# Five column tiles of each round moved between the attention units of the round before

## The chip, the core and the metric

The kernel runs on one core of one Trainium2 chip. The metric is the time of one execution on the device, in microseconds (us), lower is better; it is given as the median of several runs. The engines are TensorE (PE in the rows), VectorE (DVE), ScalarE (ACT), GpSimd (POOL) and the queue engine SyncE (SP). Each runs its own instructions in order; they meet at semaphores.

## What is computed

One layer of a hybrid decoder on 512 tokens of width 1024: three token mixing branches (dilated sliding-window attention, a convolution module, an mLSTM matrix memory) run on one input projection, are gated per channel and summed; then an output projection, a mixture of experts, a per-layer input embedding and a last norm. The change touches the token mixing alone. Attention has three dilations and eight slots of 64 channels; the convolution module is a gated input, a depthwise convolution of 31 taps, a LayerNorm and a swish; memory q and k pass a depthwise convolution of 4 taps. Cut to that:

```python
h = rmsnorm(x, g_mix[i])
proj = h @ w_in[i]
(q_a, k_a, v_a, u_conv, q_m, k_m, v_m, o_m, i_m, f_m, gate_pre) = jnp.split(proj, SPLIT_IDX, axis=-1)
y_att = dilated_attention(q_a, k_a, v_a)
y_conv = conformer_conv(u_conv, ...)
qk = jax.nn.silu(causal_dwconv(concat([q_m, k_m]), ...))
h_m = mlstm(q_c, k_c, v_m, i_m + ..., f_m + ...)
y_m = jax.nn.sigmoid(o_m) * h_m
gates = jax.nn.sigmoid(gate_pre).reshape(b, s, N_BRANCH, d)
merged = (gates[..., 0, :] * (y_att @ w_br_att[i])
          + gates[..., 1, :] * (y_conv @ w_br_conv[i])
          + gates[..., 2, :] * (y_m @ w_br_mlstm[i]))
x = x + merged @ w_out[i]
```

## The kernel before

The program has stages one behind the other: the first norm and its transposes (to 34 us of the profiled execution), four **rounds** (34 to 463), the **merge** of the three branches in eight tiles of 128 channels (to 671), the output projection and router (to 773), the experts (to 1033), and the last stage. The change touches the rounds and the start of the merge.

A round `r` computes 128 channels of every branch: two attention slots, 128 convolution channels, one memory head. Its parts, by engine:

- **Column tiles**, eight of them (`CM_ORDER`): TensorE multiplies 128 columns of `w_in` with all 512 tokens, into bank `PA` or `PB` by turns. Each product is split: the weights and `h` are given as a rounded high part and a low part (what rounding left), and three products are summed (`split_product`, L786 is `mm`), so a column tile is 8 x 3 = 24 matmuls of 512 columns. ScalarE rounds the weights (`round_cm`, L569, two buffers `cm_high`), VectorE subtracts to get the **low part** (`cm_tile`, L1219), and only then TensorE may start. Tile order: convolution gate, convolution input, memory q, memory k, three attention q, attention k.
- **Token tiles**, four: 128 tokens by 384 channels (attention v, output gate, memory v), again 24 matmuls, with weights `wtm` rounded by ScalarE (L605) and with a low part of 3072 columns.
- The **31 taps** of the depthwise convolution on VectorE (L1286), with the low parts of column tiles 4 to 7 and of the token weights laid between them at places fixed by `CM_TILES_AT` and `TM_TILE_AT`; behind them the memory convolution (L1294, L1298), eight instructions, and its swish (L1302).
- Eight **units** `u`, one for each slot and block of 128 queries: TensorE scores for three dilations (plain fp32), VectorE adds the bias and takes the maximum (L1326, L1331, `negmax_ready`), ScalarE the exponent (L619), GpSimd adds the three parts (L1621, L1623), TensorE turns them (L878), ScalarE copies (L613), TensorE multiplies with v. Units 0 to 3 have a token tile on TensorE behind their scores. Units 4 to 7 have instead one short matmul of memory scores, whose product with the weights is L1338.
- The **tail**: memory outputs (ten matmuls of 129 columns), the last turn and products, the memory rows on VectorE (L1349 to L1363), two sets of four transposes (L935, L939), copied out by ScalarE (L645, L647) into `yT`.
- GpSimd writes the ALiBi **bias** of the next round (L1607, six products) when ScalarE has done the output gate (`sgo_ready`, L642).

Round 0 is straight code on TensorE and a loop runs rounds 1 to 3; on VectorE and ScalarE a loop runs rounds 0 to 2 and the last is straight code. TensorE starts the column tiles of a round when the tail of the one before is done. VectorE makes the low parts of tiles 0 and 1 of the next round in units 4 and 5, so these alone are ready early. After round 3 the LayerNorm of the convolution branch runs: two means over channels as matmuls with `mean` (L786), subtraction (L1386), squares and root on ScalarE (L670, L672), reciprocal and four more steps on VectorE (L1393 to L1397), swish. The first merge tile is mixed with it: gate, mean, branch, gate, branch, gate, branch. The merge weights come by two loads, `wg` (1.5 MB) and `wb` (0.75 MB), on one semaphore; `wb` lies where `wtm` lies, so both loads are asked for when the last token tile is done, and ScalarE waits for both in unit 3 of round 3 before it rounds the first gate (L573).

## Time and profile before

| | us |
|---|---|
| median of three runs | 1118.33 |
| lowest, highest | 1117.27, 1120.91 |
| the profiled execution, its own time | 1119.16 |
| its span, first to last instruction | 1117.3 |
| TensorE busy | 979.6 (88%) |
| VectorE busy | 458.3 (41%) |
| ScalarE busy | 307.7 (28%) |
| GpSimd busy | 163.4 (15%) |

Busy TensorE is not TensorE at its peak: matmuls overlap, their ends are modelled, and a matmul at the lower clock is busy for longer. So the share of 88% is read together with the granted clock of each stretch, and with what stands between two matmuls. By stage the span divides into 34 us ahead of the rounds, 429 us of rounds, 208 us of LayerNorm end and merge, and 446 us behind them.

### The profile page before, as it was taken

The page shows a single profiled execution, that of the slowest core. Times are in us where ns is not written, and L with a number is a line of the kernel's source. Part 1 is how long each engine was busy: PE and PEld are TensorE (multiplying, and loading weights), DVE is VectorE, ACT ScalarE, POOL GpSimd, SP SyncE. Part 2 cuts the span into 40 slices and gives each one's busy share as a digit, 9 for nine tenths or more (in the row PEclk, how much of TensorE's full clock was granted, in tenths as well). Part 3 has the DMA queues.
Part 4 walks back from the last instruction along what each step waited for, and adds up shares of the span by engine and source line. Part 5 has one row for each costly group of instructions (what it writes and reads, how often), then busy time and mean ns, then how long its engine had stood idle before and what let it go on. Part 6 is the DMA issues. An engine that isn't in the chain of part 4 may idle for free.

```text
span 1117.3 us, 12509 instructions
## 1 busy us (share of the span) xinstructions
PE 979.6 (88%) x4614; PEld 676.0 (61%) x4614; DVE 458.3 (41%) x979; ACT 307.7 (28%) x508; POOL 163.4 (15%) x172
## 2 busy tenths in 40 slices
PE   6699999989999997999999999958888777987696
PEld 6478677867776785678888884544444343443342
DVE  5595439346842953483334321353111111111443
ACT  3332432443242333542222210112111111111233
POOL 0131330250034012000000000001222122221000
PEclk7799899979997997899999999988999889999698
DMA  5221032003201202243222207052999999996400
GB/s 210 95 63 51 1 109 80 19 1 131 75 0 39 93 0 85 84 171 150 85 85 85 85 9 311 38 218 106 385 425 428 427 412 411 402 428 275 162 38 38
DMA packets 22581, 176.27 MB, mean 158 GB/s; under 512 B 5372, under 2 KB 5756, under 8 KB 16272
## 3 DMA queue, kind: packets, MB, share of 16 engines
q1 hardware_dynamic: 17424, 167.37, 37.7%
q0 software_dynamic: 5120, 8.41, 2.0%
q8 instruction: 23, 0.38, 0.1%
q14 instruction: 14, 0.11, 0.0%
HBM read 171.55 MB, written 12.58 MB: 165 GB/s over the span
## 4 chain that ended last, share of the span: by engine, by line
PE 64%; DMA 13%; DVE 11%; issue 7%; ACT 3%; POOL 1%; DVEq 0%; SPq 0%; ACTq 0%; POOLq 0%
PE bank L786 61%; DMA mT<-normed,table 10%; DVE arena L1286 3%; DVE low_parts L1219 2%; DMA arena<-in_pT 1%; DVE arena L1326 1%; PE bank L1001 1%; DMA arena<-in_w_branch 1%; PE bank L878 1%; PE bank L1093 1%; DVE hT_parts L1214 1%; ACT yT L736 1%; DVE yT L1545 0%; DVE yT L1547 0%; PE bank L814 0%
## 5 line engine op out<-in xcount | busy, mean ns | idle before, releaser
L786 PE MATMUL bank<-arena 128*128 128x64 f32 (+7 forms) x624 | 190.3, 459 | 27.4 <-DVE arena L1310 8.9
L786 PE MATMUL bank<-arena,yT 128*64 128x256 f32 (+1 forms) x1280 | 183.6, 444 | 12.6 <-ACT yT L736 11.7
L786 PE MATMUL bank<-mT_parts,low_parts 128*128 128x512 f32 x448 | 178.2, 398 | 0.0
L786 PEld LDWEIGHTS bank<-arena 128*128 128x128 f32 (+1 forms) x624 | 111.8, 222 | 101.2 <-issue 69.7
L786 PEld LDWEIGHTS bank<-arena,yT 128*64 128x64 f32 x1280 | 92.7, 142 | 95.4 <-issue 45.3
L786 PE MATMUL bank<-mT_parts,x_parts 128*128 128x512 f32 x320 | 129.7, 405 | 17.4 <-DVE low_parts L1219 13.7
L786 PE MATMUL bank<-hT_parts,x_parts 128*128 128x512 f32 x320 | 127.8, 399 | 0.0
L1219 DVE TENSOR_TENSOR low_parts<-arena,x_parts 128x1024 fp32r<-128x1024 f32 (+1 forms) x44 | 62.3, 1416 | 129.0 <-ACT x_parts L573 100.7
L786 PEld LDWEIGHTS bank<-mT_parts,low_parts 128*128 128x128 f32 x448 | 85.3, 190 | 20.5
L1545 DVE TENSOR_TENSOR yT<-bank,yT 128x128 f32<-128x128 f32 x32 | 9.3, 292 | 192.9 <-ACT yT L731 192.9
L786 PEld LDWEIGHTS bank<-mT_parts,x_parts 128*128 128x128 f32 x320 | 61.3, 192 | 34.1 <-issue 15.7
L1286 DVE SCALAR_TENSOR_TENSOR arena<-arena,chn 128x512 f32<-128x512 f32 x116 | 80.5, 765 | 0.0
L1636 POOL DMA_INDIRECT mT<-normed,table x32 | 33.0, 1031 | 320.7 <-DVE table_weight L1532 308.7
L786 PEld LDWEIGHTS bank<-hT_parts,x_parts 128*128 128x128 f32 x320 | 61.3, 192 | 14.3 <-issue 0.2
L786 PE MATMUL bank<-arena,hT 128*128 128x512 f32 (+1 forms) x192 | 69.2, 513 | 0.8 <-DVE hT L1178 0.8
L1326 DVE CUSTOM_DVE_ANT_0 arena<-bank,arena 128x128 f32<-128x128 f32 (+3 forms) x96 | 38.7, 453 | 73.5 <-issue 61.0
L1642 POOL DMA_INDIRECT expert_rows<-mT,table x32 | 32.4, 1012 | 190.4 <-ACT mT L743 190.4
L786 PEld LDWEIGHTS bank<-arena,hT 128*128 128x128 f32 x192 | 36.5, 225 | 31.2 <-issue 30.0
L786 PE MATMUL bank<-mT_parts,cm_high_b 128*128 128x512 f32 x128 | 51.0, 399 | 3.1 <-DVE low_parts L1219 3.1
L619 ACT ACTIVATE arena<-arena,small 128x384 f32<-128x384 f32 (+3 forms) x32 | 32.5, 1015 | 72.1 <-DVE small L1331 72.1
L786 PE MATMUL bank<-hT_parts,cm_high_b 128*128 128x512 f32 x128 | 50.3, 393 | 0.0
L1621 POOL TENSOR_TENSOR arena<-arena 128x128 f32<-128x128 f32 (+3 forms) x32 | 31.7, 991 | 125.1 <-ACT arena L619 125.1
(242 smaller groups left out, 1234.4 us busy)
## 6 DMA issues: line engine op xcount, KB each, us to landing
arena<-in_w_expert SPq DMA_DIRECT2D x32, 3072.0 KB, 15.5
arena<-in_w_cm SPq DMA_DIRECT2D x32, 512.0 KB, 3.6
arena<-in_w_gate SPq DMA_DIRECT2D x8, 1536.0 KB, 6.4
arena<-in_w_tm SPq DMA_DIRECT2D x4, 1536.0 KB, 6.8
arena<-in_w_branch SPq DMA_DIRECT2D x8, 768.0 KB, 7.9
x_sb<-in_x SPq DMA_DIRECT2D x8, 512.0 KB, 4.7
arena<-in_w_out SPq DMA_DIRECT2D x1, 4096.0 KB, 12.2
arena<-in_w_pg SPq DMA_DIRECT2D x2, 2048.0 KB, 11.5
```

Of the source, the lines that this page charges most:

```text
L619: act.activation(sc[:, u % 2, 0:n], sc[:, u % 2, 0:n], ACT.Exp, bias=nmx[:, u % 2:u % 2 + 1], accum_out=den[:, u:u + 1]).then_inc(exps_don ...
L736: act.activation(hx[b2], HT[:, 0:P].rearrange("p (j s) -> p j s", j=2), ACT.Copy).then_inc(hx_ready, 1)
L786: return pe.matmul(out, lhsT, rhs, start=start, stop=stop)
L878: last = pe.transpose(TR[:, j * P:(j + 1) * P], psm[:, u % 2, j * P:(j + 1) * P], ident)
L1001: last = pe.transpose((S_16, OUT)[half][:, k * P:(k + 1) * P], x_sb[:, t, (4 * half + k) * P:(4 * half + k + 1) * P], ident)
L1093: pe.transpose(HT[:, 0:P], hs[b2], ident).then_inc(h_turned, 1)
L1219: dve.tensor_tensor(low, weights, high.bitcast(F32), ALU.subtract).then_inc(done, 1)
L1286: dve.scalar_tensor_tensor(cacc[:, j % 2], ypad[:, j:j + SEQ], w31(j), cacc[:, j % 2], ALU.mult, ALU.add).then_inc(conv_step, 1)
L1326: dve.tensor_tensor_reduce(out=sc[:, u % 2, at:at + width], in0=bank[:, 0:width], in1=bias[:, s, b0:b0 + width], scale=1.0, scalar=-3e38, ...
L1621: pool.tensor_tensor(dst[:, 0:n], sc[:, u % 2, 0:n], sc[:, u % 2, n:2 * n], ALU.add).then_inc(pool_step, 1)
L1636: pool.indirect_dma_start(out=xr[slot], out_offset=None, in_=normed_halves, in_offset=bass.IndirectOffsetOnAxis(ap=token_halves, axis=0), ...
L1642: pool.indirect_dma_start(out=expert_halves, out_offset=bass.IndirectOffsetOnAxis(ap=row_halves, axis=0), in_=yr[slot], in_offset=None, bo ...
```

## The change

The loops over rounds are unrolled on all engines, and the parts are functions that are called in a new order.

- **Rotation.** Column tiles 0 to 4 of round r+1 are computed in units 3 to 7 of round r, one in each, behind the scores. Round 0's own tiles 0 to 4 come first, without cover. Then each round has tile 5, the memory outputs of the round before, tile 6, its last product and memory transposes, tile 7, its attention transposes, token tile 0, and the units. Token tile 0 thus stands ahead of unit 0's scores, tiles 1 to 3 in units 0 to 2.
- **Tile order.** Now memory q and k first, then convolution gate and input, then the attention tiles. The convolution gate is copied out of its bank raw (`gate_out`) and made a sigmoid later, in unit 7 (`open_gate`, semaphore `gate_open`), together with the output gate, which has a place of its own (`sgo`) instead of sharing `sgt`.
- **VectorE.** The taps are split: 15 in the part between the units (`projections`), the others in the units by `CONV_IN_UNIT`; in round 3 by `CONV_LAST_ROUND`, so that all are done in unit 3. Low parts of tiles 0 to 4 are made in units 2 to 6, tile 5 behind unit 7, tiles 6 and 7 and the token weights among the taps. The memory convolution has a semaphore of its own.
- **Last round.** Instead of column tiles, TensorE does the first mean in unit 4, the second in unit 5, merge gate 0 in unit 6 and merge gate 1 in unit 7 (`last_round_filler`); squares, root, reciprocal and the rest of the LayerNorm are laid among the units on ScalarE and VectorE. Behind the tail come gate 2 and three branches of merge tile 0.
- **Merge.** Branch order is memory, attention, convolution; banks are `PA`, `PB`, `S_16` for gates and `S_1`, `S_4`, `OUT` for branches. `wg` and `wb` have separate semaphores; the first `wg` load is asked for when the last column tile is done. From merge tile 1 on the order is as before.

The diff, cut to that:

```diff
-        CM_TILES_AT = {8: 4, 14: 5, 22: 6, 28: 7}
-        TM_AFTER, TM_TILE_AT = 4, 10
+        TM_AFTER = 6
+        CONV_IN_UNIT = (15, 18, 21, 23, 25, 27, 29, 30, 31)
+        CONV_LAST_ROUND = (15, 20, 25, 29, 31, 31, 31, 31, 31)
...
             sp.wait_ge(cm_done, CM_CREDIT + ROUNDS * CM_ORDER)
+            gate_weights(0, 0)
             sp.wait_ge(tm_done, ROUNDS * T)
-            merge_weights(0, 0)
+            branch_weights(0, 0)
...
+            for r in range(ROUNDS):
+                column_tile(r, 5)
+                if r:
+                    memory_out(r - 1)
+                column_tile(r, 6)
+                if r:
+                    memory_turn(r - 1)
+                column_tile(r, 7)
+                if r:
+                    attention_turn(r - 1)
+                token_tile(r, 0)
+                units(r)
+            memory_out(ROUNDS - 1)
+            memory_turn(ROUNDS - 1)
+            attention_turn(ROUNDS - 1)
+            merge_gate(0, 2)
...
                 for u in range(8):
+                    scores(r, u)
+                    if u >= T:
+                        memory_scores(r, u - T)
+                    if u < T - 1:
+                        token_tile(r, u + 1)
+                    elif r + 1 < ROUNDS:
+                        column_tile(r + 1, u + 1 - T)
                     else:
+                        last_round_filler(u)
                     if u >= 2:
+                        pv(r, u - 2)
                     if u >= 1:
+                        turn(r, u - 1)
...
+            def projections(r):
+
+                gated_input(r)
+                cm_tile(r, 6)
+                memory_conv(r)
+                conv_steps(r, 0, 4)
+                if r:
+                    memory_rows(r - 1)
+                memory_swish(r)
+                cm_tile(r, 7)
+                conv_steps(r, 4, 7)
+                if r:
+                    out_of_slot(r - 1, 1)
+                conv_steps(r, 7, 9)
+                low_part(wtm_high, wtm_low, wtm, r * (CM_ORDER + 1) + TM_AFTER + 1, tm_split)
+                conv_steps(r, 9, CONV_IN_UNIT[0])
...
+                    if 2 <= u < 7:
+                        cm_tile(r + 1, u - 2)
+                    conv_steps(r, CONV_IN_UNIT[u], CONV_IN_UNIT[u + 1])
+                cm_tile(r + 1, 5)
```

What stands in a row now. TensorE in units 5 and 6 of round 0, before: a turn and a product, the scores of unit 6 with one matmul of memory scores, product and turn, and the scores of unit 7.

```order
L786 MATMUL bank<-arena 128x64 x4
L878 MATMUL bank<-cst,arena 128x128
L786 MATMUL bank<-arena 128x256
L786 MATMUL bank<-arena 128x384 x2
L786 MATMUL bank<-arena 128x256
L786 MATMUL bank<-arena 128x64
L878 MATMUL bank<-cst,arena 128x128 x2
L786 MATMUL bank<-arena 128x256
L786 MATMUL bank<-arena 128x512 x2
```

The same place after, up to the first products of column tile 3 of round 1 (of which there are 24, over `mT_parts`, `hT_parts` and `low_parts`):

```order
L877 MATMUL bank<-arena 128x64 x4
L976 MATMUL bank<-cst,arena 128x128
L877 MATMUL bank<-arena 128x256
L877 MATMUL bank<-arena 128x384 x2
L877 MATMUL bank<-arena 128x256
L877 MATMUL bank<-mT_parts,cm_high_b 128x512
L877 MATMUL bank<-hT_parts,cm_high_b 128x512
L877 MATMUL bank<-mT_parts,low_parts 128x512
```

A whole column tile has moved between the scores of a unit and the product and turn of earlier ones.

VectorE behind unit 7 before: memory product (L1338), the memory rows (L1349 to L1363) and the output step of the second slot, then the next round.

```order
L1338 TENSOR_TENSOR arena<-bank,arena 128x128
L1349 COPY md<-bank 128x2 x2
L1352 ISA
L1353 SCALAR_TENSOR_TENSOR md<-md 128x4
```

After, from the same memory product (L1517) on: the last tap and the sum, the low part of tile 5, the gated input (L1422), the low part of tile 6, and the memory convolution (L1431, L1435).

```order
L1517 TENSOR_TENSOR arena<-bank,arena 128x128
L1412 SCALAR_TENSOR_TENSOR arena<-arena,chn 128x512
L1416 TENSOR_TENSOR yT<-arena 128x512
L1362 TENSOR_TENSOR low_parts<-arena,cm_high_b 128x1024
L1422 TENSOR_TENSOR arena<-bank,arena 128x512
L1362 TENSOR_TENSOR low_parts<-arena,x_parts 128x1024
L1431 TENSOR_SCALAR arena<-arena,chn 128x512
L1435 SCALAR_TENSOR_TENSOR arena<-arena,chn 128x512 x3
L1431 TENSOR_SCALAR arena<-arena,chn 128x512
L1435 SCALAR_TENSOR_TENSOR arena<-arena,chn 128x512 x3
L1406 TENSOR_SCALAR arena<-arena,chn 128x512
L1409 TENSOR_SCALAR arena<-arena,chn 128x512
```

The memory rows (L1459 to L1473) follow two taps behind this, and the swish and the low part of tile 7 behind them.

VectorE in round 3 between unit 6 and unit 7, after (before, these LayerNorm steps L1391 to L1397 stand in the merge, behind the attention):

```order
L1517 TENSOR_TENSOR arena<-bank,arena 128x256
L1549 TENSOR_SCALAR arena<-bank 128x512
L1551 RECIPROCAL arena<-arena 128x512
L1552 TENSOR_TENSOR arena<-arena 128x512
L1553 TENSOR_TENSOR arena<-arena 128x512
L1554 TENSOR_SCALAR arena<-arena 128x512
L1555 TENSOR_TENSOR arena<-arena 128x512
L1502 MEMSET takes_wait 1x1
L1505 ISA arena,small<-bank,arena 128x512
```

L1505 there is the bias of unit 7, which now stands behind the reciprocal.

## Rows read from the trace of the kernel before

**Rows 1.** Second and last round: us; busy (x count) of PE, PEld, DVE, ACT, POOL; PEclk, DMA.

```profile
148.00:250.50 102.50, 95.54 (x433) 75.40 (x433) 57.02 (x133) 37.57 (x60) 22.90 (x26) 0.93 0.17 57
...
353.00:463.00 110.00, 98.14 (x433) 76.25 (x434) 57.66 (x134) 36.95 (x59) 15.01 (x19) 0.89 0.15 55
```

**Rows 2.** Stretches of the second round and of the merge, same columns.

```profile
147.84:195.67 47.83, 45.36 (x192) 35.85 (x193) 35.48 (x46) 14.23 (x17) 1.78 (x2) 1.00 0.33 110
195.67:221.24 25.57, 25.57 (x133) 22.00 (x133) 8.40 (x37) 9.94 (x19) 6.80 (x9) 1.00 0.06 21
221.24:250.46 29.22, 24.73 (x109) 17.67 (x109) 13.15 (x51) 13.51 (x26) 14.44 (x16) 0.77 0.00 1
...
496.10:671.40 175.30, 175.17 (x757) 141.88 (x756) 59.73 (x78) 40.14 (x58) 0.00 (x0) 1.00 0.25 97
```

**Rows 3.** Chain of waits, in time: start us, us, what.

```profile
94.49 11.19 PE bank L786 x60
...
195.67 11.27 PE bank L786 x60
...
250.46 11.43 PE bank L786 x48
...
400.52 11.27 PE bank L786 x60
...
425.81 7.64 DMA arena<-in_w_branch
...
493.31 177.97 PE bank L786 x768
```

**Rows 4.** Timeline of TensorE, second round: start, us, line, count, [idle before <-releaser].

```profile
213.72 2.41 PE L786 MATMUL bank<-arena 64*128 64x256 f32 x6
...
232.16 0.69 PE L786 MATMUL bank<-arena 128*128 128x64 f32 x2 [2.05 <-DVE arena L1310]
...
245.46 0.61 PE L878 MATMUL bank<-cst,arena 128*128 128x128 f32 x4
```

**Rows 5.** VectorE by line, 147.8 to 250.4: count | busy, mean ns | idle before.

```profile
L1286 DVE SCALAR_TENSOR_TENSOR arena<-arena,chn 128x512 f32<-128x512 f32 x29 | 19.8, 754 | 0.0
...
L1219 DVE TENSOR_TENSOR low_parts<-arena,x_parts 128x1024 fp32r<-128x1024 f32 (+1 forms) x5 | 8.2, 1650 | 9.2 <-ACT x_parts L569 9.2
L1219 DVE TENSOR_TENSOR low_parts<-arena,cm_high_b 128x1024 fp32r<-128x1024 f32 x4 | 4.9, 1224 | 3.9 <-ACT cm_high_b L569 3.9
L1298 DVE SCALAR_TENSOR_TENSOR arena<-arena,chn 128x512 f32<-128x512 f32 x6 | 4.5, 752 | 0.9 <-DVE arena L1294 0.2 <-DVE arena L1298 0.2
...
L1302 DVE SCALAR_TENSOR_TENSOR arena<-arena 128x512 f32<-128x512 f32 x2 | 1.4, 690 | 0.1
...
L1363 DVE SCALAR_TENSOR_TENSOR arena<-bank,md,arena 128x128 f32<-128x128 f32 x4 | 1.1, 346 | 0.1
```

**Rows 6.** ScalarE by line, same stretch.

```profile
L569 ACT ACTIVATE cm_high_b<-arena 128x1024 fp32r<-128x1024 f32 x4 | 4.2, 1056 | 4.0 <-PE bank L786 4.0
...
L642 ACT ACT_TABLE_LOAD x1 | 1.3, 1283 | 0.0
```

**Rows 7.** Timeline of GpSimd: bias products (L1607) and two first additions (L1621).

```profile
57.92 8.61 POOL L1607 TENSOR_SCALAR arena<-cst,slope_now 128x256 f32<-128x256 f32 x6
...
200.69 0.46 POOL L1621 TENSOR_TENSOR arena<-arena 128x128 f32<-128x128 f32 x1 [0.36 <-ACT arena L619]
...
224.14 1.36 POOL L1621 TENSOR_TENSOR arena<-arena 128x128 f32<-128x128 f32 x1 [2.46 <-ACT arena L619]
...
244.24 7.97 POOL L1607 TENSOR_SCALAR arena<-cst,slope_now 128x256 f32<-128x256 f32 x6
```

**Rows 8.** Timeline of VectorE: taps in rounds 0 and 1, the reciprocal.

```profile
60.60 5.59 DVE L1286 SCALAR_TENSOR_TENSOR arena<-arena,chn 128x512 f32<-128x512 f32 x6
...
163.34 4.06 DVE L1286 SCALAR_TENSOR_TENSOR arena<-arena,chn 128x512 f32<-128x512 f32 x6
...
476.92 3.35 DVE L1393 RECIPROCAL arena<-arena 128x512 f32<-128x512 f32 x1 [0.70 <-ACT arena L672]
```

More of the change, by code:

```diff
@@ L58 @@
 FREE = 1
-CONV_STEPS = CONV_K + 2 * MCONV_K
+MCONV_STEPS = 2 * MCONV_K
 MAX_OVER = (2 * SEQ - NEXP) // BLK
@@ new lines, in column_tile @@
+            def column_tile(r, n):
+                pe.wait_ge(cm_split, r * CM_ORDER + n + 1)
+                pe.wait_ge(bank_read[n % 2], FREE + 6 * r + n // 2)
+                for k in range(KD):
+                    if r == 0 and n == 0:
+                        pe.wait_ge(h_split[k >= H_DVE], k + 1 - H_DVE * (k >= H_DVE))
+                    part = slice(k * P, (k + 1) * P)
+                    last = split_product((PA, PB)[n % 2][:, :], cm_high[n % 2][:, part], wcm_low[:, n % 4, part],
+                                         h_high[:, k, :], h_low[:, k, :], k == 0, k == KD - 1)
+                last.then_inc(cm_done, 1)
@@ new lines, in token_tile @@
+            def token_tile(r, u):
+                if u == 0:
+                    pe.wait_ge(tm_split, r + 1)
+                pe.wait_ge(bank_read[u % 2], FREE + 6 * r + 4 + u // 2)
+                for k in range(KD):
+                    part = slice(u * P, (u + 1) * P)
+                    last = split_product((PA, PB)[u % 2][:, 0:3 * P], h_high[:, k, part], h_low[:, k, part],
+                                         wtm_high[:, k, :], wtm_low[:, k, :], k == 0, k == KD - 1)
+                last.then_inc(tm_done, 1)
@@ new lines, in memory_scores, with conv_mean @@
+            def memory_scores(r, j):
+                if j == 0:
+                    pe.wait_ge(qk_ready, 2 * (r + 1))
+                    pe.wait_ge(y_ready, FREE + 2 * r)
+                else:
+                    pe.wait_ge(m_weighted, r * T + j)
+                mm(MM[:, 0:(T - j) * P], qk[:, 1, j * P:(j + 1) * P], qk[:, 0, j * P:]).then_inc(m_scores, 1)
+            def conv_mean(bank, terms):
+                for c in range(ROUNDS):
+                    last = mm(bank[:, :], const("mean"), terms[:, c, :], c == 0, c == ROUNDS - 1)
+                last.then_inc(ln_mm, 1)
@@ new lines, in merge_gate @@
+            def merge_gate(dt, br):
+                s = dt % 2
+                pe.wait_ge(gate_split, 3 * dt + br + 1)
+                if dt:
+                    pe.wait_ge(gate_read, 3 * (dt - 1) + br + 1)
+                for k in range(KD):
+                    part = slice(k * P, (k + 1) * P)
+                    last = split_product((PA, PB, S_16)[br][:, :], gate_high[br][:, part], wg_low[s][:, br, part],
+                                         h_high[:, k, :], h_low[:, k, :], k == 0, k == KD - 1)
+                last.then_inc(gate_done, 1)
@@ L940, in one_round @@
                 last.then_inc(att_turned, 1)
-                pe.wait_ge(y_ready, FREE + 2 * r + 1)
-            one_round(0, first=True)
-            with pe.Fori(1, ROUNDS) as r:
-                one_round(r)
-            pe.wait_ge(conv_ready, ROUNDS)
-            for c in range(ROUNDS):
-                last = mm(TR[:, :], const("mean"), yT[:, 2, c, :], c == 0, c == ROUNDS - 1)
-            last.then_inc(ln_mm, 1)
-            for b in range(2):
-                pe.wait_ge(bank_read[b], FREE + 6 * ROUNDS)
@@ L1373, in branch_low @@
+            for n in range(2, 5):
+                cm_tile(0, n)
+            cm_tile(0, 5)
+            for r in range(ROUNDS - 1):
+                projections(r)
+                units(r)
+            projections(ROUNDS - 1)
+            last_units(ROUNDS - 1)
             def branch_low(dt, br):
```

657 lines of the change are left out of this document (369 added, 288 removed).

## The prediction

> **What bounds the kernel now.** I read the table of whole rounds first: TensorE busy 95.5 of 102.5 us and 98.1 of 110 us, at a mean clock of 0.93 and 0.89 [rows 1], where the merge behind them has 1.00 [rows 2]. Then the stretches of the second round [rows 2]: its eight column tiles take 47.8 us with TensorE busy 45.4; units 0 to 3, each with a token tile, 25.57 us with TensorE busy all the time; units 4 to 7 and the tail 29.22 us with TensorE busy 24.73 at a mean clock of 0.77. There TensorE has only small products, each behind a step of another engine: it waits 2.05 us for one VectorE step [rows 4], and its clock is at the lower level (1.2 GHz) for part of the stretch. Last the chain of waits [rows 3]: units begin at 94.49, 195.67 and 400.52, so three rounds take 306.0 us, nearly all of it on TensorE; the last round has 7.64 us of a weight load in the chain; from 493.31 on 768 products run back to back, 0.2317 us each. A column tile is 24 of them, 5.57 us (two took 11.43). The merge stretch is bound by TensorE alone [rows 2]; the change leaves it alone.
>
> **One period, counted for TensorE at full clock.** A period runs from unit 0 of a round to unit 0 of the next, 102.0 us on average before. Its work: eight column tiles 8 x 5.57 = 44.6; units 0 to 3 with four token tiles 25.6 [rows 2]; and the rest. The rest has 6,026 columns of plain fp32 products (scores 3,456, memory scores 1,280, memory outputs 1,290); 1,280 columns took 2.41 us [rows 4], so 11.3 us; and 39 small ones (17 probability products, 22 transposes) at about 0.16 (four transposes took 0.61 [rows 4]), 6.4 us. Sum 17.7. The other side: busy 24.73 times clock 0.77 is 19.0, an upper bound, since busy spans overlap. I take 17.7, since it counts what must run; period 87.9, with 89.2 as its upper end. So 14 us of each period are waits and low clock, and that is what five column tiles laid between the small steps can give back.
>
> **What hides the small steps in units 3 to 7.** A unit now lasts about 8.4 us on TensorE (scores, memory scores, one column tile, probability product, turn). Meanwhile VectorE has its bias (1.9 at most), memory product 0.7, one low part 1.2, one or two taps at 0.66, some 5 us; ScalarE an exponent, two weights, two copies and a rounding 1.06 [rows 6], some 4.5. Each column tile is rounded a unit and a half before TensorE asks for it. So I cost these units no wait. The 7.64 us for branch weights [rows 3] goes too: rounding needs only the gate weights, and these are asked for before the token tiles.
>
> **What is late next: column tile 7 and the token tile.** Count from the scores of unit 7. TensorE could start tile 5 at 9.0, tile 6 at 18.0 (behind memory outputs and a turn) and tile 7 at 25.0. ScalarE ends its exponent at 5.7, loads a table (1.28), opens the gate, does the out gate, copies tile 4 and has tile 6 rounded at 9.7. From there VectorE goes in one row: low part 1.15, memory convolution 6.3 (two starts, six taps, gaps), four taps 2.2, memory rows 2.6, swish 1.4, low part of tile 7 1.15: 14.8 us by its rows [rows 5], so 24.5. Alone that would cost nothing.
>
> But GpSimd's six bias products now start when the out gate is done, at about 8.5, and lie beside this row. Before, in rounds 1 to 3 they lay where VectorE idled (7.97 us [rows 7]); in round 0 they lay beside taps, and there six taps took 5.59 where six took 4.06, and GpSimd 8.61 [rows 7, 8]: 1.5 us over six taps. The row has about ten such instructions beside the bias products, so 2.6 us. I give back 0.5 because the unrolled taps need no register instructions (between 0 and 0.064 each: a tap's mean is 754 ns, the swish, of the same kind and size without them, 690 [rows 5]). Tile 7 then starts at 26.6, wait 1.6. Behind it VectorE has five taps, an output step and the token low part (8.2 minus four of 1.22, 3.3 [rows 5]), 7.1 in all, to 33.7; TensorE asks at 32.9: wait 0.9. Bounds of the two waits: 0 (no contention) and 7.5. Period 87.9 + 2.5 = 90.4; three are 271.2 against 306.0.
>
> How hard the two engines meet is open: a GpSimd addition that takes 0.46 alone took 1.36 beside a low part [rows 7], as if it had stood still for it, while in the bias products both engines ran on, each some tenths slower. The Trainium skill ("SBUF — State Buffer", section "SBUF: two separate sides") says that the port pair which VectorE and GpSimd share is an exclusive lock: whoever starts first has it for the whole instruction and the other fully blocks. By that rule, the addition agrees and the bias products do not; with it the two waits would be 7.9 us together and the sum 1099.
>
> **Head and end.** Round 0: the same row of VectorE work starts when tile 6 is rounded, and that is behind the copy of tile 4, at 76.9: tile 7 waits 2.7, the token tile about 1, and 1.8 of short gaps go. Unit 0 begins at 94.5 + 4.4 (the token tile now stands ahead) + 1.9 = 100.8. Last round, from unit 0 to the second merge tile (before 400.52 to 496.1, less the token tile, 91.2): work 21.2 + 17.7 + two means 6.2 + three gates 16.7 + three branches 8.4 = 70.2. Waits that I find: 1.6 ahead of unit 4's scores and the mean; 5.5 ahead of the second mean, since the squares follow the subtractions, a bias, an exponent and a rounding; with that gap the clock falls, as it fell around a gap of 2.05 (in the second round it was low for 2 x 0.23 x 29.22 = 13 us [rows 2]); I take 10 us at half speed, cost 5. The reciprocal of the deviations (3.35 [rows 8]) and its four companions, 6 us, now stand ahead of VectorE's bias 7; behind that bias wait exponent 7, copy, turn and memory outputs: 4 to 6 more. Sum 88; bounds 80 and 98.
>
> **The sum.** 100.8 + 271.2 + 88.0 = 460.0 where the merge from its second tile on started at 496.1. Merge 175.3 and the rest, 671.4 to 1117.3, stay as they are: span 1081.2, and with the 1.9 us around the span 1083. The profiled execution took 1119.16, the median of three 1118.33: the same within 0.1%.
>
> **Rivals.**
> - Clean: GpSimd and VectorE hardly meet and the clock stays up. For it: VectorE waits a little ahead of that row. Three periods at 87.9, end 5 shorter: 1070.
> - The clock falls in each rotation: a wait of 1.6 to 2 us ahead of tile 7 is as long as the gap of 2.05 beside which it fell [rows 4], though the column tiles' stretch, with 2.5 us of short gaps, stands at 1.00 [rows 2]. Tile 7, a turn and the token tile, 10.7 us, at half speed, less the wait they cover: 4 a period, 1095.
> - VectorE is shut out for the whole of the bias products: 8.0 a period where I took 2.6, so 5.4 more, 1099. The Trainium skill's page named above has this as its rule.
> - The last round holds more: attention's end stands behind the LayerNorm row with the clock low throughout, 10 more: 1093.
> - Slower: the column tiles' two rounding buffers turn into a wait. TensorE serves in order, so a low part that comes late holds the scores behind it, and with them the bias, which stands ahead of the next low part on VectorE. It decides once VectorE's load in a unit passes TensorE's 8.4; at 5 it does not. If each of five tiles then waits for a bias (1.3), a rounding and a low part in turn, 3.6 us [rows 5, 6], a period is 108.4: 1137.
> - It doesn't act: the new instruction order shows the tiles between the units, so this stays at 2 in 100, 1118.
>
> **How the numbers follow.** Forecast 0.45, clean 0.17, clock 0.15, last round 0.10, shut out 0.07, slower 0.04, no effect 0.02. Likeliest 1083. The range 1068 to 1098 takes in the first four; 0.13 is left out by mechanism and a little by spread. A difference of 0.3% (3.4 us) is about what a measurement tells from none: faster 0.94, same 0.02, slower 0.04.
>
> **What would show it.** In the profile after, units begin every 90 us or so and TensorE's clock is at 1.00 from unit 3 to tile 6 of each rotation. The wait ahead of tile 7 is named VectorE's low part, 1 to 2 us, and the memory convolution beside GpSimd's bias takes 8 to 9 us instead of 6.3. In the last round a gap of about 5 us stands before the second mean. The prediction is wrong if column tiles in units 4 to 7 start after a wait for a low part, if merge products stop being back to back, or if tile 7 never waits.

## The result and the profile after

| | before | after |
|---|---|---|
| median, us | 1119.62 | 1081.76 |
| lowest, highest | 1117.27, 1122.67 | 1076.19, 1088.21 |
| the profiled execution, its span | 1117.3 | 1079.1 |
| from unit 0 to unit 0 of the next round, mean | 102.0 | 90.0 |
| unit 0 of the last round to the second merge tile | 95.6, without its token tile 91.2 | 88.1 |
| VectorE, GpSimd busy | 458.3, 163.4 | 480.1, 190.3 |

The changed kernel takes 0.966 of the time before, with a 95% interval of 0.960 to 0.972. The forecast of 1083 lies 1.2 us from the median; its mechanism holds, three of its smaller terms do not, and errors of opposite sign bring the number closer than its parts are, as the runs below show.

Whole stretches of the changed kernel: from and to, length, then the busy time of TensorE, its weight loads, VectorE, ScalarE and GpSimd, the granted clock, and the DMA share. The first three are the rounds, to be held against [rows 1] and [rows 2]; the fourth is the last round from its first scores, the fifth the merge. The cut between these two, at 461.00, is 0.7 us early: the second merge tile starts at 461.72.

```profile
99.18:189.19 90.01, 88.19 (x432) 71.33 (x432) 63.37 (x134) 36.31 (x59) 30.73 (x25) 1.00 0.20 66
189.19:279.16 89.97, 88.16 (x432) 71.30 (x432) 63.38 (x134) 36.31 (x59) 30.72 (x25) 1.00 0.19 65
279.16:369.14 89.98, 88.16 (x432) 71.30 (x433) 63.39 (x134) 36.31 (x59) 30.74 (x25) 1.00 0.15 49
373.58:461.00 87.42, 77.25 (x338) 57.71 (x338) 62.85 (x138) 44.59 (x73) 15.31 (x16) 0.90 0.17 68
461.00:636.84 175.84, 175.82 (x760) 142.31 (x758) 59.20 (x76) 40.14 (x58) 0.00 (x0) 1.00 0.24 93
```

A round now is 90.0 us long with TensorE busy for 88.2 of them at a clock of 1.00, where two rounds had 0.93 and 0.89. From its second tile on the merge is unchanged (175.1 us from 461.72, 175.3 in [rows 2]). The chain of waits of the changed kernel (start, length, what) over one period and from there to the merge, beside [rows 3]:

```profile
189.19 15.59 PE bank L877 x84
...
257.47 0.93 DVE arena L1431
...
271.15 1.57 DVE arena L1412 x2
272.72 0.52 issue
...
275.84 3.28 DVE low_parts L1362
...
279.16 15.59 PE bank L877 x84
...
409.87 2.09 ACT arena L719 x4
...
426.15 3.36 DVE arena L1551
...
446.76 190.07 PE bank L877 x816
```

From 189.19 to 254 the chain is TensorE alone, from token tile 0 over the units to column tile 5. Then it follows VectorE's row (memory convolution from 257.47, low part of tile 7 until 271.15, token low part until 279.12). The load of 7.64 us is gone. What TensorE itself waits for is in its timeline (the brackets hold the idle time ahead and what ended it):

```profile
279.16 0.44 PE L877 MATMUL bank<-x_parts,mT_parts 128*128 128x384 f32 x1 [1.70 <-DVE low_parts L1362]
...
412.09 5.23 PE L877 MATMUL bank<-arena,cst 128*128 128x512 f32 x8 [5.17 <-ACT arena L719]
...
439.79 0.88 PE L877 MATMUL bank<-arena 128*128 128x64 f32 x6 [1.70 <-ACT arena L626]
...
443.09 1.97 PE L877 MATMUL bank<-arena 128*128 128x64 f32 x8 [1.98 <-ACT arena L626]
```

In a period the timeline shows one wait, 1.70 us ahead of the first token tile (the same at 189.19 and 369.14). Ahead of column tile 7 no bracket stands in rounds 1 to 3, but a short wait is there all the same, 0.36 us, as the run without bias products shows below.

What follows the merge, from the row of 64 products to the end, took 444.4 us before and 440.6 after. Nothing there was changed; in the other profiles it took 438.7 to 449.1, with gathers of 22 to 31 us of DMA in the chain. A difference of medians below 5 us is therefore read from the trace up to the merge as well. Below, "period" is the mean over three rounds, counted from first scores to first scores, and "last stretch" runs from the last round's first scores to the second merge tile; where a token tile lies inside, it is said. A token tile is 4.4 us. The kernel before was run again beside each group of runs (medians 1122.05 to 1122.47), and the ratios are to those.

### The profile page after: what moved, and what is told of

It is laid out like the page before. It is cut to its first block, busy times and chain, and to the rows that moved or that the text cites. A ratio compares the mean times of both kernels' runs of the same rounds, so it can differ in the third digit from the quotient of the medians.

```text
span 1079.1 us, 11975 instructions
## 1 busy us (share of the span) xinstructions
PE 955.1 (89%) x4614; PEld 663.8 (62%) x4614; DVE 480.1 (44%) x980; ACT 306.2 (28%) x512; POOL 190.3 (18%) x172
## 4 chain that ended last, share of the span: by engine, by line
PE 68%; DMA 13%; DVE 12%; ACT 4%; issue 2%; POOL 0%; SPq 0%; ACTq 0%; POOLq 0%; DVEq 0%
PE bank L877 65%; DMA mT<-normed,table 10%; DVE arena L1412 2%; DVE low_parts L1362 2%; DVE arena L1435 2%; DMA arena<-in_pT 1%; PE bank L1144 1%; PE bank L1236 1%; DVE hT_parts L1357 1%; DVE arena L1431 1%; ACT yT L827 1%; PE bank L905 1%; PE bank L976 0%; DVE arena L1505 0%; DMA x_sb<-in_x 0%
## 5 line engine op out<-in xcount | busy, mean ns | idle before, releaser
L877 PE MATMUL bank<-arena,yT 128*64 128x256 f32 (+1 forms) x1280 | 179.6, 436 | 12.6 <-ACT yT L827 11.7
L877 PE MATMUL bank<-arena 128*128 128x64 f32 (+7 forms) x624 | 170.8, 416 | 11.9 <-DMA arena<-in_pT 5.4
L877 PEld LDWEIGHTS bank<-arena 128*128 128x128 f32 (+1 forms) x624 | 98.9, 192 | 75.4 <-issue 57.1
L1412 DVE SCALAR_TENSOR_TENSOR arena<-arena,chn 128x512 f32<-128x512 f32 x116 | 99.8, 911 | 0.0
L1821 POOL TENSOR_TENSOR arena<-arena 128x128 f32<-128x128 f32 (+3 forms) x32 | 40.2, 1258 | 223.2 <-ACT arena L657 223.2
L877 PE MATMUL bank<-arena,hT 128*128 128x512 f32 (+1 forms) x192 | 71.7, 527 | 0.8 <-DVE hT L1321 0.8
L877 PEld LDWEIGHTS bank<-arena,hT 128*128 128x128 f32 x192 | 38.9, 243 | 31.3 <-issue 30.1
L877 PE MATMUL bank<-x_parts,mT_parts 128*128 128x384 f32 x128 | 44.9, 351 | 6.7 <-DVE low_parts L1362 6.7
```

The lines of the kernel that those rows point to most:

```text
L877: return pe.matmul(out, lhsT, rhs, start=start, stop=stop)
L1412: dve.scalar_tensor_tensor(cacc[:, j % 2], ypad[:, j:j + SEQ], weight, cacc[:, j % 2], ALU.mult, ALU.add).then_inc(conv_step, 1)
L1821: pool.tensor_tensor(dst[:, 0:n], sc[:, u % 2, 0:n], sc[:, u % 2, n:2 * n], ALU.add).then_inc(pool_step, 1)
```

## The experiments

| kernel | median | ratio to before, 95% | period | last stretch |
|---|---|---|---|---|
| e1_unrolled | 1117.64 | 0.9959 (0.9931 to 0.9988) | 100.2 | 96.9, token tile inside |
| e2_no_rotation | 1144.99 | 1.0209 (1.0171 to 1.0247) | 109.8 | 85.9 |
| e9_no_rotation_tokens | 1111.87 | 0.9915 (0.9886 to 0.9944) | 100.2 | 89.4, token tile inside |
| e3_no_filler | 1091.25 | 0.9754 (0.9718 to 0.9789) | 90.0 | 93.6 |
| e6_split_loads | 1122.89 | 1.0023 (1.0002 to 1.0044) | 102.0 | 94.6, token tile inside |
| e10_early_gate | 1115.38 | 0.9934 (0.9907 to 0.9960) | 102.4 | 88.1, token tile inside |
| e0_after | 1083.68 | 0.9656 (0.9626 to 0.9686) | 90.05 | 87.3 |
| e5_no_pool_bias | 1075.69 | 0.9607 (0.9571 to 0.9644) | 88.5 | 88.2 |
| e11_late_tile7 | 1093.94 | 0.9760 (0.9699 to 0.9822) | 92.4 | 86.6 |
| e4_early_token | 1069.56 | 0.9548 (0.9516 to 0.9581) | 88.1 | 86.5 |
| e8_both | 1068.62 | 0.9535 (0.9510 to 0.9560) | 88.1 | 79.7 |

The last round and what follows it to the second merge tile are the same on TensorE in e0_after, e2, e4, e5, e11 and the changed kernel, and took 85.9 to 88.2 us there. So differences of 2 us in the last column are not read.

**Is it the unrolling?** The kernel before, loops written out:

```diff
-            with pe.Fori(1, ROUNDS) as r:
+            for r in range(1, ROUNDS):
```

> The kernel before with its round loops written out four times and nothing else changed: no instruction moves. Theory (the gain lies in the column tiles between the units): writing out saves only register and loop instructions. A tap's mean was 754 ns where the swish of the same kind took 690, so at most 0.064 us for each of some 116 taps, and nearly all of them lie in VectorE's idle time: 0 to 5 us, so 1114 to 1119. Rival (the loops' own instructions are a large part of what TensorE waits for, since 7% of the chain before stood under issue and 2% after): 15 us or more faster, 1104 or less.

Measured 0.9959, some 4.6 us. The period falls by 1.8 us (102.0 to 100.2), three of them are 5.5. This is the upper end of what I gave to it; the rival is out. Windows of this kernel, two periods, each cut 0.8 us ahead of unit 0's scores, columns as above:

```profile
196.50:298.00 101.50, 95.34 (x432) 75.19 (x432) 57.12 (x134) 36.23 (x58) 22.76 (x25) 0.93 0.18 58
298.00:398.30 100.30, 94.10 (x432) 73.99 (x432) 56.56 (x134) 36.13 (x59) 22.81 (x25) 0.95 0.13 43
```

**Is it the rotation?** The changed kernel with column tiles 0 to 4 behind the tail:

```diff
-                    elif r + 1 < ROUNDS:
-                        column_tile(r + 1, u + 1 - T)
...
+                    memory_out(r - 1)
+                    memory_turn(r - 1)
+                    attention_turn(r - 1)
+                    for n in range(5):
+                        column_tile(r, n)
```

> The changed kernel with column tiles 0 to 4 of the next round taken out of units 3 to 7 and put behind the round's tail, with their roundings, low parts and copies; the written-out loops, the split loads and the filled last round stay. Theory: the waits and the lower clock of units 4 to 7 and of the tail come back, 8 to 12 us in each of three periods: 24 to 36 us slower than the changed kernel, 1106 to 1118, units about 98 to 102 us apart, granted clock under 0.95 over the rounds. Rival (the new order of vector work and the unrolling made the gain): within 10 us of the changed kernel, 1082 to 1092, periods under 94.

It is slower than the kernel before, by 2.1%: 61 us above the changed kernel, twice what I had expected. The direction is that of the theory, the size is not. Its windows (a period, cut at its first token tile, and in it units 4 to 7 with the tail):

```profile
209.60:319.10 109.50, 101.76 (x432) 78.89 (x432) 61.03 (x134) 36.87 (x59) 25.68 (x25) 0.88 0.17 54
...
236.59:270.70 34.11, 31.14 (x109) 21.38 (x110) 19.32 (x59) 12.45 (x24) 14.69 (x16) 0.60 0.00 1
```

The clock of 0.60 stands in a stretch in which TensorE has only small steps, and here unit 3, ahead of it, has only small steps too: the change has moved every token tile one unit ahead, so without column tiles five units are empty, not four. This could be tried: token tile u back in unit u.

```diff
-                    if u < T - 1:
-                        token_tile(r, u + 1)
+                    if u < T:
+                        token_tile(r, u)
```

> As the run without rotation, but with token tile u inside unit u, as in the kernel before; so only units 4 to 7 and the tail are unfilled, where the run without rotation left unit 3 empty as well. Theory (what counts is how many of the units hold a big tile): the period falls from 109.5 back to 99 to 102 us, the kernel stands at the written-out kernel's time or up to 5 us under it (the last round is filled): 1095 to 1115, granted clock of a period 0.93 to 0.97. Rival (the changed order of VectorE's and ScalarE's work costs by itself what the run without rotation showed): a period of 106 us or more, 1130 or slower.

The period falls to 100.2, that of the written-out kernel, and the clock is 0.93, 0.95 and 0.95 in the three periods. So the new order of VectorE's and ScalarE's work, without the rotation, gives and costs nothing in sum (its single waits differ: 1.99 us ahead of column tile 7, where the written-out kernel has 0.82 and 0.62 ahead of two tiles); the step from 100.2 to 90.0 belongs to the big tiles between the small steps, and one more empty unit costs 9.6 us a round. A row of this kernel beside the one above:

```profile
201.95:301.42 99.47, 93.78 (x433) 74.55 (x433) 58.78 (x132) 36.73 (x60) 25.81 (x25) 0.95 0.18 59
```

**What is the last round's filling worth?** LayerNorm's means and the two gates back behind the tail:

```diff
-                    else:
-                        last_round_filler(u)
...
+            conv_mean(TR, yT[:, 2])
+            merge_gate(0, 0)
+            pe.wait_ge(ln_act, ROUNDS)
+            conv_mean(MM, lnt)
+            merge_gate(0, 1)
             merge_gate(0, 2)
```

> The changed kernel with the last round's filling undone: LayerNorm's means, its vector work and the first two merge gates stand behind the tail, as before; the rotation and the split loads stay. From the rows: the stretch from unit 0 of the last round to the second merge tile was 91.2 us before (without the token tile), 7.64 of it the weight load that is gone now, so 83.6, where the changed kernel takes 87.1. By that count the filling is worth nothing or costs 3 us: 1077 to 1082. Rival (the filling pays, since without it units 4 to 7 wait 2 us each at the lower clock, and the weight load only hid such waits): 6 to 12 us slower, 1087 to 1093.

The rival was right in kind: 93.6 us instead of 88.1 (87.3 in the second profile of the changed kernel), 5.4 to 6.3 us, and 0.9754 against 0.9656 in time. The 87.1 in the expectation was counted with all products behind the tail at full clock; six of them ran at the lower level, and the second merge tile starts at 461.72, which makes 88.1. The count had also left out that unit 3 lost its token tile. From unit 4 to the end of the tail, without the filling and, second, in the changed kernel, where two means and two gates, 17.3 us of work, lie inside:

```profile
396.13:432.27 36.14, 31.03 (x109) 21.02 (x109) 19.11 (x59) 18.59 (x33) 9.86 (x10) 0.62 0.00 0
```

```profile
396.02:446.41 50.39, 41.38 (x172) 28.25 (x173) 31.95 (x73) 25.75 (x42) 9.30 (x10) 0.86 0.00 0
```

**What ended the 7.64 us wait for weights?** First one semaphore each for gate and branch weights in the kernel before, then also the gate weights asked for behind the last column tile:

```diff
-                sp.dma_start(wb[slot], w_branch[dt, :, :, :]).then_inc(mw_loaded[slot], 16)
+                sp.dma_start(wb[slot], w_branch[dt, :, :, :]).then_inc(bw_loaded[slot], 16)
```

```diff
+            gate_weights(0, 0)
             sp.wait_ge(tm_done, ROUNDS * T)
-            merge_weights(0, 0)
+            branch_weights(0, 0)
```

> The kernel before with one semaphore for the gate weights and one for the branch weights, so that the first gate's rounding no longer waits for the branch weights; nothing else is changed. Theory: the 7.64 us that the chain showed for that load go, less what is late next (a rounding of 1.06 and a copy): 5 to 8 us faster, 1111 to 1114. Rival (another step ends the same wait): less than 2 us, 1117 to 1120.

> The kernel before with split semaphores and, now, the first gate weights asked for behind the last column tile instead of behind the last token tile. With the semaphores split alone the chain still held 6.03 us, now of the gate weights' own load. Theory (the load's start was the cause): no load stands in the chain, the merge's row of 768 products begins 6 to 8 us earlier than in the kernel before (493.3), the median is 0.4 to 0.7% under it. Rival (the small steps beside it, at the lower clock, end the same wait): under 2 us.

Splitting alone gains nothing in time, and 1.0 us in the stretch. Its chain shows why: the wait now ends with the gate weights' own load, which landed 30.9 us behind scores 0, where before the branch weights landed at 32.9 [rows 3].

```profile
428.92 6.03 DMA arena<-in_w_gate
```

With the earlier request no load stands in the chain, and the stretch from scores 0 to the branch products is 85.3 us where it was 92.8 [rows 3]:

```profile
405.17 11.19 PE bank L796 x60
...
490.43 177.95 PE bank L796 x768
```

That is 7.5 us, and the median is 0.66% (7.4 us) under that of before. So the late request was what the split alone left standing. The early request with the one shared semaphore was not run; there the branch weights, which lie where the token weights lie and so can't be asked for earlier, would still be waited for. Set against this, the last stretch of before less the load is 88.0, without its token tile 83.6, and the changed kernel has 88.1 (kernels with the same last round 85.9 to 88.2), so its last round is 2 to 5 us longer than that of before would be. Without filling it is 93.6, about 10 above 83.6; that kernel differs from e10_early_gate in more than the token tiles' place, so that these cost the 10 us is likely and not shown. The filling brings 5 to 8 of them back. Where the token tile stays in unit 3 (e9_no_rotation_tokens), the filled stretch is 85.0 without that tile, so there the filling brought nothing that shows beside 83.6.

**How much do GpSimd and VectorE disturb each other?** Beside the changed kernel itself once more, one with the bias products of rounds 1 to 3 cut to one column:

```diff
+                        n = n if r == 0 else 1
-                        pool.tensor_scalar(bias[:, s, at:at + n], const(name),
+                        pool.tensor_scalar(bias[:, s, at:at + n], const(name)[:, 0:n],
```

> The changed kernel itself once more, as the baseline beside which the next ones are read. Expected: ratio to the kernel before 0.966 (0.960 to 0.972), a period of 90.0 us, and 1.70 us of wait ahead of the first token tile of each round.

> The changed kernel, with GpSimd's six bias products of rounds 1 to 3 cut to one column each; the position bias of those rounds is left out, so their attention is another one. It prices the meeting of GpSimd and VectorE. Theory (both run on, VectorE's instructions each some tenths longer): the memory convolution falls from 6.8 to 6.3 us, the taps behind it from about 0.9 to 0.75, the wait ahead of the token tile from 1.70 to 0 to 0.7, a period to 88.3 to 89.0, 3 to 5 us in all. Rival A (the wait does not come from the meeting but from the length of VectorE's row): the period stays at 90.0. Rival B (GpSimd shuts VectorE out for whole instructions): the row falls by 5 us or more and memory convolution with it to under 5.

Timeline of VectorE's memory convolution in e0_after (a start and three taps, for each of two rows), and of the bias products:

```profile
256.32 0.92 DVE L1431 TENSOR_SCALAR arena<-arena,chn 128x512 f32<-128x512 f32 x1
257.27 2.64 DVE L1435 SCALAR_TENSOR_TENSOR arena<-arena,chn 128x512 f32<-128x512 f32 x3
...
264.35 1.41 DVE L1412 SCALAR_TENSOR_TENSOR arena<-arena,chn 128x512 f32<-128x512 f32 x2
```

```profile
254.59 10.30 POOL L1807 TENSOR_SCALAR arena<-cst,slope_now 128x256 f32<-128x256 f32 x6
```

and the same place of e5_no_pool_bias:

```profile
256.32 0.54 DVE L1431 TENSOR_SCALAR arena<-arena,chn 128x512 f32<-128x512 f32 x1
256.90 2.33 DVE L1435 SCALAR_TENSOR_TENSOR arena<-arena,chn 128x512 f32<-128x512 f32 x3
...
262.82 1.41 DVE L1412 SCALAR_TENSOR_TENSOR arena<-arena,chn 128x512 f32<-128x512 f32 x2
```

The row is 1.5 us shorter (taps begin at 262.82 instead of 264.35), and the whole of it reaches the end: the period falls from 90.05 to 88.5. The wait ahead of the token tile gives 1.2 of that (1.70 to 0.54). The rest is a wait ahead of column tile 7 that is too short for a bracket. TensorE's last transposes before that tile and its first product, in e0_after and, second, in e5_no_pool_bias:

```profile
269.32 0.61 PE L1086 MATMUL bank<-cst,arena 128*128 128x128 f32 x4
270.05 0.50 PE L877 MATMUL bank<-mT_parts,cm_high_b 128*128 128x512 f32 x1
```

```profile
269.33 0.61 PE L1086 MATMUL bank<-cst,arena 128*128 128x128 f32 x4
269.69 0.48 PE L877 MATMUL bank<-mT_parts,cm_high_b 128*128 128x512 f32 x1
```

The product follows 0.73 us behind the transposes' start, 0.36 when VectorE's low part is early: a wait of 0.36 us, in every round of the changed kernel (0.72 to 0.74). So the meeting costs 1.5 us a period, not 2.6. Outside this row a tap beside one of GpSimd's additions takes longer as well (1.50 us at 243.39 in the changed kernel, 0.75 at 250.80 with GpSimd idle), but lies in VectorE's slack. Rival B is out for the bias products: GpSimd's six products, 7.97 us beside an idle VectorE [rows 7], took 10.30 while VectorE worked nearly throughout. The Trainium skill ("SBUF — State Buffer", section "SBUF: two separate sides") has the pair of ports that the two share as an exclusive lock with the loser fully blocked, on VectorE's side for instructions with two inputs in SBUF, as the taps and the low part are; for this pair the trace does not agree, since 7.97 us of GpSimd and about 6.9 us of VectorE (a low part, two starts and six taps at the durations of e5_no_pool_bias; 5.8 without the starts, which have one input there) passed within the same 10.30 us.

**Is the token wait needed?** The low part of the token weights three taps earlier:

```diff
-                conv_steps(r, 4, 7)
+                conv_steps(r, 4, 6)
                 if r:
                     out_of_slot(r - 1, 1)
-                conv_steps(r, 7, 9)
                 low_part(wtm_high, wtm_low, wtm, r * (CM_ORDER + 1) + TM_AFTER + 1, tm_split)
-                conv_steps(r, 9, CONV_IN_UNIT[0])
+                conv_steps(r, 6, CONV_IN_UNIT[0])
```

> The changed kernel with one VectorE order altered: the low part of the token weights stands three taps earlier (behind two taps and the output step instead of five and the output step). Theory (the 1.70 us wait ahead of the first token tile is that low part's alone): three taps are 2.7 us at 0.911 us each, so the wait goes in all four rounds, a period is 88.3 and the last stretch begins 1.6 + 3 x 1.7 = 6.7 us earlier: about 0.6% under the changed kernel. Rival (the wait only moves, to the output turn or into the units, where the taps now pile up): a period of 89.5 to 90.0, less than 2 us in all.

No wait is left in a period but the 0.36 us ahead of column tile 7; the rest is TensorE's work:

```profile
101.87:190.03 88.16, 88.04 (x434) 71.44 (x433) 63.15 (x134) 36.31 (x59) 30.74 (x25) 1.00 0.20 66
190.03:278.10 88.07, 87.95 (x433) 71.35 (x432) 63.24 (x134) 36.31 (x59) 30.74 (x25) 1.00 0.20 67
```

The row that follows the attention turn of the last round (816 products) begins at 438.81 instead of 444.51. The ratio, 0.9548, stands clear of the changed kernel's 0.9656: 1.1% faster than it, of which the trace accounts for 7.0 us, 0.6%, up to the end of the merge (629.50 instead of 636.50); the rest of the difference lies behind it, where nothing was changed (439.4 and 444.3 us in the two profiles).

**Does a short gap cost the clock?** One of the forecast's rivals. The low part of column tile 7 placed three taps later:

```diff
-                cm_tile(r, 7)
                 conv_steps(r, 4, 7)
+                cm_tile(r, 7)
```

> The changed kernel with the low part of column tile 7 three taps later on VectorE, so that TensorE meets a wait of about 2.0 us ahead of that tile, with the tile and a token tile behind it. VectorE's row keeps its length, so the later wait ahead of the token tile (1.70) shrinks by as much. Theory of the forecast (a short gap amid column tiles leaves the clock up): a period of 90.0 to 90.6. Rival (the clock falls behind a gap of 2 us): products behind it at 0.43 to 0.46 us each instead of 0.23, a period of 92 to 94, 6 to 12 us in all.

The gap became 2.95 us, since the three taps take 2.9 and tile 7 had no slack before them. TensorE's timeline behind it:

```profile
279.71 0.80 PE L877 MATMUL bank<-mT_parts,cm_high_b 128*128 128x512 f32 x1 [2.95 <-DVE low_parts L1362]
280.31 0.63 PE L877 MATMUL bank<-hT_parts,cm_high_b 128*128 128x512 f32 x1
...
282.44 0.57 PE L877 MATMUL bank<-mT_parts,cm_high_b 128*128 128x512 f32 x1
282.85 0.40 PE L877 MATMUL bank<-hT_parts,cm_high_b 128*128 128x512 f32 x1
```

Products start 0.43 us apart, at a granted clock of 0.50 (the 1.2 GHz level), and from 282.85 on 0.23 apart at 1.00: the clock did fall, in the midst of column tiles and in each of the rounds, and about seven products paid 0.2 each, 1.4 us. With the gap that makes 4.3 on 88.1, 92.4, and 92.4 is the period measured. The median is 10 us above that of the changed kernel. So the rival's mechanism exists, the theory that a short gap is harmless falls, and the price of the clock is a third of the 4 us that I gave it; behind the gap of 1.70 ahead of a token tile the products ran at full pace and the period's clock was 1.00.

**Can the last round be shorter?** The early token low part, and in the last round the first gate in unit 5, the second mean in unit 6 and the reciprocal chain behind the bias of unit 7; ScalarE's last copy of probabilities also moves ahead of its four sigmoids for the LayerNorm's swish:

```diff
                 if u == 5:
+                    pe.wait_ge(ln_step, ROUNDS)
+                    merge_gate(0, 0)
+                if u == 6:
                     pe.wait_ge(bank_read[1], FREE + 6 * ROUNDS)
                     pe.wait_ge(ln_act, ROUNDS)
                     conv_mean(PB, lnt)
-                if u == 6:
-                    pe.wait_ge(ln_step, ROUNDS)
-                    merge_gate(0, 0)
```

> The early token low part and, in the last round, another order: the first merge gate fills unit 5, the second mean stands in unit 6 and the chain behind it (reciprocal and four products) behind the bias of unit 7; the attention outputs' VectorE work stands ahead of the first branch's rounding rests. Theory: the gap of 5.17 us ahead of the second mean falls to 0 to 2, the two waits of 1.70 and 1.98 ahead of the last probability products go with the chain, and 1 to 2 us come up ahead of the memory turn or the last branch: 4 to 7 us less, on top of 6.7: 11 to 14 us under the changed kernel, about 1.1%. Rival (LayerNorm's row then ends too late and the third branch waits for it): 3 to 6 us of wait ahead of that branch, so no more than the early low part's own gain.

TensorE's timeline of this kernel: the second mean stands at 407.58 with no wait, and the waits of the tail are

```profile
424.62 1.10 PE L877 MATMUL bank<-arena 128*128 128x64 f32 x8 [0.69 <-ACT arena L626]
426.56 0.66 PE L1086 MATMUL bank<-cst,arena 128*128 128x128 f32 x4 [0.84 <-DVE arena L1473]
...
428.23 0.50 PE L877 MATMUL bank<-mT_parts,x_parts 128*128 128x512 f32 x1 [0.47 <-DVE low_parts L1362]
441.74 0.47 PE L877 MATMUL bank<-y_parts 128*128 128x512 f32 x1 [2.12 <-DVE low_parts L1572]
```

The last stretch is 79.7 us instead of 86.5, and the merge ends 6.6 us earlier (622.95 and 629.50). In the median only 1 us of it shows (0.9535 against 0.9548, intervals that overlap), so between these two the time does not decide; against the changed kernel, 0.9656, both are faster. A new wait of 2.12 us stands ahead of the third branch, as the rival had it, but smaller.

## Why the prediction was right, step by step

- **What bounds the kernel** (waits and the lower clock of units 4 to 7 and the tail, 14 us a period): right. With the token wait gone a period takes 88.1 us at a clock of 1.00 (e4_early_token), 0.36 of it the wait ahead of tile 7, so 87.7 of work, where the count from rows had given 87.9 (its 39 small steps of 0.16 make 6.2, not 6.4, so it should have said 87.7). Before, a period took 102.0. Of the 12.0 between them 1.8 belong to the written-out loops and 10.2 to the rotation.
- **Column tiles between the units wait for nothing**: right, the chain from 189.19 to 254 is TensorE alone.
- **The wait ahead of column tile 7, 1.6 us**: mis-sized, it was 0.36. The forecast's sign "if tile 7 never waits" is just missed, and another of its signs did not come: the memory convolution took 6.8 us beside the bias products, not 8 to 9. Two terms failed. The contention was put at 2.6 us and measured 1.5. And the row was counted at 14.8 us without contention, where 14.9 passed with it (tile 6 rounded at 256.2, low part ready at 271.15). The memory convolution alone is 5.65 us, not 6.3, in e5_no_pool_bias and in e1_unrolled, so the written-out code gives 0.65 there. Memory rows took 1.9 instead of 2.6 (2.4 in e1_unrolled, so 0.2 of that is the writing out) and the swish 1.2 instead of 1.4 (1.4 in e1_unrolled too); why the rest went stays open. In round 0 the wait was 1.98, not 2.7.
- **The wait ahead of the token tile, 0.9 us**: it was 1.70. From low part to low part VectorE took 7.97 us, not 7.1; a pause of 0.52 between two taps (the chain's issue at 272.72) had not been counted, and the taps took 3.6, not 3.3. The errors of these two waits have opposite signs: 2.5 forecast, 2.1 measured, so that the period of 90.4 came out as 90.0 is in part luck. Three periods: 269.98 instead of 271.2.
- **Unrolling, 0.5 us a period**: too small. By itself it took 1.8 off a period of before. How much of that is left in the changed kernel, where TensorE waits for VectorE at two places only, was not measured.
- **The load of branch weights goes, 7.64 us**: right, and measured alone at 7.5. The text gives both reasons, the rounding that waits for the gate weights alone and their early request; e10_early_gate has both, and the first alone (e6_split_loads) took 1.0 us off the stretch.
- **The last round, 88 us**: 88.1, with parts that differ. The gap ahead of the second mean was 5.17 for 5.5, the wait ahead of unit 4 1.16 for 1.6. The waits put down to the reciprocal chain were 3.7 us (1.70 and 1.98) for "4 to 6", and the chain is not their only cause: ahead of the second stand ScalarE's four sigmoids, 2.82 us at 439.73 in the chain. Both waits fell to 0.69 us in all where chain and sigmoids stood elsewhere (e8_both), which doesn't part the two. With the 70.2 of counted work these waits leave 7.9 us, where the forecast had 5 for the lower clock.
- **Head**: unit 0 was forecast at 100.8 and stood at 103.6. The first column tile started at 37.74 in the changed kernel and at 34.24 in the profile of before, but between 37.5 and 38.6 in the eleven others, kernels of the old order among them; so 3.5 us belong to the early start of that one execution, and the rest was 0.7 too high. Behind the second merge tile 617.4 us passed where the forecast had 621.2, in stages whose work is the same. That the span came out 2.1 us from the forecast is luck in so far as these two, 2.8 too little and 3.8 too much, cancel.
- **Rivals**: a fall of the clock in the rotation did not come; why not is open, since the clock fell behind a gap of 1.99 us in two rounds of e9_no_rotation_tokens and did not in two others (last section). Brought about by a gap of 2.95, it cost 1.4 us. Shutting out is refuted for the bias products. "Slower by turns in the rounding buffers" did not occur.

The sum: three periods 36.0 us shorter, the last stretch 7.5 (4.4 of it the token tile, which now stands ahead), the head 9.1 longer (the same 4.4, 3.5 of the start, 1.2 of its own), merge and rest 3.8 shorter: 38.2, the difference of the spans.

## What to carry to other kernels

Big independent products laid between the small steps of a dependent chain pay twice, by the waits they cover and by the clock that they hold up; but check each step that the same edit shifts, since here the token tiles, moved by one unit, left unit 3 of the last round empty, and that round, filled, is still 2 to 5 us longer than the one before would be without its load. When an engine's row is the only one that reaches the end, list what it does ahead of each handover and put first what someone waits for: three taps moved behind a low part were worth 7.0 us in the trace, 0.6%. Where a load ends a wait, look first at when it was asked for, then at the semaphore.

## What the hardware showed unexpectedly

- The clock fell behind single gaps between big products at full pace: behind 2.95 us between column tiles, where products ran at the lower level from 279.71 to 282.85 (e11_late_tile7), and behind 2.12 us ahead of the third branch, where they ran 0.43 apart from 442.75 until 446.11 (e8_both). Behind gaps of 1.70 ahead of token tiles it did not fall. The length of the gap does not tell it. In e9_no_rotation_tokens the same gap of 1.99 us stands ahead of column tile 7 in all four rounds, and the stretch behind it was granted 0.52, 0.67, 1.00 and 1.00 (in the second round the products ran 0.23 apart at first and 0.43 apart from 195.16 on); what decides between them no run shows.

```profile
92.45:95.98 3.53, 3.53 (x9) 2.79 (x9) 3.53 (x5) 0.00 (x0) 0.90 (x1) 0.52 0.29 110
193.78:197.00 3.22, 3.22 (x10) 2.56 (x11) 3.22 (x4) 0.00 (x0) 0.89 (x1) 0.67 0.34 137
294.80:298.00 3.20, 3.19 (x14) 2.62 (x15) 3.20 (x4) 0.00 (x0) 0.91 (x1) 1.00 0.27 108
394.60:398.00 3.40, 3.33 (x14) 2.74 (x15) 3.40 (x5) 0.00 (x0) 0.96 (x1) 1.00 0.00 0
```

- In the changed kernel's tail, with small products between gaps of 1.70 and 1.98, the clock was at the lower level:

```profile
443.10:447.00 3.90, 3.90 (x18) 3.67 (x19) 2.35 (x7) 1.48 (x3) 0.00 (x0) 0.50 0.00 0
```

- GpSimd's bias product of a single column took a mean of 680 ns (e5_no_pool_bias), and a full one of 256 or 512 columns 1733 (e0_after), both beside VectorE's work; an addition of one element took 184. What the 680 are made of stays open. This also means that e5_no_pool_bias did not take the meeting away fully.
- GpSimd's memory mask (L1811) took 2.00 us where it had taken 1.10 in the kernel before: in the changed kernel it lies beside a low part and taps (270.10, where VectorE has these from 269.93 on).
